# A hybrid decoder layer on eight cores: weight casts in small pieces, early tiles in idle buffers, the mix stored alone, a new memory map for phase two

## The reference

```python
h = layer_norm(concat([meta, x]), ln_emb_g, ln_emb_b)      # 16 meta tokens + 8192 tokens, 1024 wide
hq, hf, hi, hg, aq, ak, av, gates = split(h @ w_in)        # one input projection
y_hg  = hgrn2_mixer(hq, hf, hi, hg, ...) @ w_branch_hg     # gated linear recurrence, 4 heads, chunks of 128
y_att = swa_sink_attention(aq, ak, av, ...) @ w_branch_attn  # window 128, meta tokens and a sink always seen
g_hg, g_att = split(sigmoid(gates))
mix = (g_hg * y_hg + g_att * y_att) @ w_out
h = layer_norm(ALPHA * h + mix, ln1_g, ln1_b)
a, u = split(h @ w_ffn_in)                                 # 1024 -> 2 x 2816
h = layer_norm(ALPHA * h + (silu(a) * u) @ w_ffn_out, ln2_g, ln2_b)
```

## Time and profile before

| | |
|---|---|
| Three runs | 3938.48, 4109.31, 4582.92 us (median 4109.31) |
| Profiled execution | 3938.09 us |
| Its span, slowest core | 3936.5 us |
| Spans of the eight cores | 3900.2 to 3936.5 us |
| Busy share of the span | TensorE 92%, VectorE 56%, ScalarE 31%, GpSimd 23% |

### The profile page before, as it was taken

How to read it: one execution, slowest core, us unless ns; L and a number is a source line. 1 busy time by engine, 2 the same in 40 slices (tenths; PEclk the granted TensorE clock), 3 DMA queues, 4 the chain that set the end, 5 groups by cost and what they waited for, 6 DMA issues and landing times.

```text
span 3936.5 us, 46968 instructions; the slowest of 8 cores (3900.2 to 3936.5 us)
## 1 busy us (share of the span) xinstructions
PE 3629.1 (92%) x17838; PEld 1638.3 (42%) x17838; DVE 2185.5 (56%) x2962; ACT 1233.6 (31%) x1981; POOL 899.1 (23%) x907
## 2 busy tenths in 40 slices
PE   1368989999999999999988999999999999999998
PEld 0133443444444444444433444444444444444443
DVE  2476766667777777776544444434544443444433
ACT  2254444445545555555422111111111111111110
POOL 1223332333333343333221111101111110111100
PEclk8679999999999999999999999999999999999999
DMA  8746766766676666665556444455555444555532
GB/s 154 146 119 155 194 170 177 183 188 177 198 195 173 177 193 186 185 183 164 157 190 189 145 149 140 132 152 161 156 149 145 146 132 145 155 165 145 149 114 81
DMA packets 405412, 631.01 MB, mean 160 GB/s; under 512 B 270482, under 2 KB 279842, under 8 KB 403908
## 3 DMA queue, kind: packets, MB, share of 16 engines
q1 hardware_dynamic: 400628, 597.59, 52.9%
q0 software_dynamic: 4560, 30.41, 5.4%
HBM read 495.60 MB, written 126.35 MB: 158 GB/s over the span
## 4 chain that ended last, share of the span: by engine, by line
PE 74%; DMA 10%; DVE 9%; ACT 3%; issue 2%; POOL 2%; SPq 1%; DVEq 0%; POOLq 0%; ACTq 0%
PE ps L1329 27%; PE ps L1352 15%; PE ps L90 8%; PE ps L1089 8%; PE ps L947 4%; PE ps L1127 4%; PE ps L801 3%; DMA xB_78<-h_scr 2%; PE ps L1106 2%; DMA ring<-wgb_bf 2%; DMA xA_77<-x 2%; PE ps L1103 1%; PE ps L773 1%; DVE rd L90 1%; DVE m_149 L90 1%
## 5 line engine op out<-in xcount | busy, mean ns | idle before, releaser
L1352 PE MATMUL ps<-wfo,gT 128*128 128x512 bf16 x2736 | 603.6, 379 | 0.0
L1329 PE MATMUL ps<-h1T_166,ring 128*128 128x512 bf16 x2482 | 592.4, 380 | 0.0
L1329 PE MATMUL ps<-h1T_167,ring 128*128 128x512 bf16 x2480 | 590.1, 379 | 0.0
L1352 PEld LDWEIGHTS ps<-wfo,gT 128*128 128x128 bf16 x2736 | 267.7, 98 | 322.8
L1329 PEld LDWEIGHTS ps<-h1T_166,ring 128*128 128x128 bf16 x2482 | 243.4, 98 | 294.6 <-issue 3.2
L1329 PEld LDWEIGHTS ps<-h1T_167,ring 128*128 128x128 bf16 x2480 | 242.7, 98 | 292.6
L90 POOL TENSOR_SCALAR rs_54<-mv_50 128x1 f32<-128x1 f32 x32 | 40.9, 1278 | 1142.1 <-DVE mv_50 L90 1142.1
L90 POOL TENSOR_TENSOR mT<-m_149 128x512 bf16<-128x512 f32 x128 | 174.8, 1365 | 463.4 <-DVE m_149 L90 371.9
L90 DVE RECIPROCAL rd<-ps 128x512 f32<-128x512 f32 x64 | 214.3, 3348 | 38.8 <-PE ps L1063 38.7
L90 DVE TENSOR_TENSOR gT<-sl_169,ps 128x512 bf16<-128x512 f32 x128 | 87.7, 686 | 263.0 <-PE ps L1329 261.9
L90 ACT ACTIVATE sl_169<-ps 128x512 f32<-128x512 f32 x128 | 76.4, 597 | 494.1 <-PE ps L1329 494.1
(11 more groups left out here) (535 smaller groups left out, 6185.1 us busy)
## 6 DMA issues: line engine op xcount, KB each, us to landing
ring<-wfi_bf SPq DMA_DIRECT2D x352, 512.0 KB, 3.7
ring<-wgb_bf SPq DMA_DIRECT2D x128, 768.0 KB, 5.9
xA_77<-x SPq DMA_DIRECT2D x64, 512.0 KB, 5.1
h_scr<-xA_77 SPq DMA_DIRECT2D x64, 512.0 KB, 3.6
ring<-wqf_bf SPq DMA_DIRECT2D x64, 512.0 KB, 5.7
xB_78<-h_scr SPq DMA_DIRECT2D x64, 512.0 KB, 4.3
r_scr<-xB_78 SPq DMA_DIRECT2D x64, 512.0 KB, 2.8
wfi_bf<-w_fi POOLq DMA_DIRECT2D x22, 512.0 KB, 7.4
```

Of the source, the lines that this page charges most:

```text
L1329: inst = e.matmul(bank(P, k)[:, 0:ntok], w[:, c * 256 + k * 128:c * 256 + (k + 1) * 128], h1T[g % 2][:, c, 0:ntok], start=(c == 0), stop=( ...
L1352: inst = e.matmul(bank(P, n), gT[:, gslots[j], s * 128:(s + 1) * 128], wfo[:, j, n * 512:(n + 1) * 512], start=(j == 0), stop=(j == NJ - 1))
```

## The change

- A cast is split: `cast_tile` and `cast_rows` cut each weight into pieces of 256 KB of fp32 (128 KB of bf16; `wo` in pieces of twice that). Still four are in flight, now four pieces. The order is `wakv`, `waq`, two heads of `wqf`, `wv`, `whg`, the other two heads, then as before. 25 casts ahead of the FFN weights become 92, the 44 of the FFN weights 132.
- The first x tile is loaded ahead of all else. `xA` has two buffers; in the first two groups stage 0 also uses `ogT[1]` and `aoT[1]`, which are idle then, so four x tiles can be loaded at once. `hbf` and `og` fall from two buffers to one; the meta tokens' `kdm` shares `A_sb[0]`.
- Stage 5 no longer loads h: ScalarE copies the scaled product to `xB`, which is stored to `r_scr`. Stage 6 loads h and the mix (`mx`, two buffers), and GpSimd adds them.
- In a normalisation the addition of eps moves from GpSimd to VectorE (also for `ss` of the recurrence); the power stays on GpSimd.
- The map of phase two puts `h1` and `h1T` on `wv`, `whg`, `waq`, `wakv`, `th`, `qd`, and `wfo` at the end, on `wo`, `xB`, `mT` and their neighbours.
- `WIN`: stage 2 ends at 0.9, stage 5 runs from 0.5 to 0.8, stage 0 from 0.6 to 0.95.

```diff
-NXA, NXB, NHB = 1, 1, 2
+NXA, NHB, NOG = 2, 1, 1
...
-WIN = {"2": (0, 1), "3": (0, 1), "12": (0, 1), "4": (0, 0.5), "5": (0.6, 1), "0": (0.5, 1)}
+WIN = {"2": (0, 0.9), "3": (0, 1), "12": (0, 1), "4": (0, 0.5), "5": (0.5, 0.8), "0": (0.6, 0.95)}
...
+    kdm, Bkdm = A_sb[0], BA[0]
+    x0 = [(xA[0], [BxA[0]]), (xA[1], [BxA[1]]),
+          (ogT[1][:].rearrange("p h t -> p (h t)").bitcast(F32), BogT[1]),
+          (aoT[1][:].rearrange("p h t -> p (h t)").bitcast(F32), BaoT[1])]
...
+    NH1 = 8
+    h1, Bh1 = sbn("h1", [128, D], F32, NH1)
+    h1T, Bh1T = partsn("h1T", [128, 8, 512], BF16, 4, 2)
+    h1b, Bh1b = sbn("h1b", [128, D], BF16, 2)
+    mx, Bmx = sbn("mx", [128, D], F32, 2)
...
+    place["at"] = (limit - NJ * 2048) // 32 * 32
+    wfo, Bwfo = sb("wfo", [128, NJ, 1024], BF16, NJ)
...
+    def cast_tile(t, src, Bs, ncol):
+
+        n = 8 // len(Bs)
+        for k, b in enumerate(Bs):
+            cast_dma(t[:, k * n:(k + 1) * n, :].rearrange("p c n -> p (c n)"), src[:, k * n * ncol:(k + 1) * n * ncol],
+                     [b], n * ncol * 512)
+
+    def cast_rows(dst, src, Bs, ncol, after=()):
+
+        n = 128 // len(Bs)
+        for k, b in enumerate(Bs):
+            cast_dma(dst[k * n:(k + 1) * n, :], src[k * n:(k + 1) * n, :], [b], n * ncol * 4, after)
...
-        S.op("pool", lambda e: e.tensor_scalar(out=rs[i][p0:p1, :], in0=mv[i][p0:p1, 1:2], scalar1=eps, scalar2=None,
-                                               op0=ALU.add), [Bmv[i]], [Brs[i]], cost=200)
+        S.op("dve", lambda e: e.tensor_scalar(out=rs[i][p0:p1, :], in0=mv[i][p0:p1, 1:2], scalar1=eps, scalar2=None,
+                                              op0=ALU.add), [Bmv[i]], [Brs[i]], cost=160)
...
-        k = t % NXA
+        k = s if g < 2 else s % NXA
...
-        dma(lambda e: e.dma_start(out=xb[:], in_=h_d[t * 128:(t + 1) * 128, :]), [Bh_d[t]], [Bxb], "hl%d" % k, 524288)
...
-            S.op("pe", fw(n), BmT + [Bwo, Bxb], [P.sub[n]], cost=MM(8))
-        S.op("dve", lambda e: e.scalar_tensor_tensor(out=xb[:], in0=pair(P), scalar=0.5 / ALPHA, in1=xb[:],
-                                                     op0=ALU.mult, op1=ALU.add), P.sub + [Bxb], [Bxb],
-             cost=dve(1024))
+            S.op("pe", fw(n), BmT + Bwo, [P.sub[n]], cost=MM(8))
+        S.op("act", lambda e: e.activation(out=xB[:], in_=pair(P), func=AF.Copy, scale=0.5 / ALPHA), P.sub, [BxB],
+             cost=act(1024))
...
+    cast_tile(wakv, w_akv, Bwakv, 256)
+    cast_tile(waq, w_aq, Bwaq, 512)
+    cast_rows(wqf_d[0], w_qf[0], Bwqf[0], 2048)
+    cast_rows(wqf_d[1], w_qf[1], Bwqf[1], 2048)
+    cast_tile(wv, w_v, Bwv, 512)
+    cast_tile(whg, w_hg, Bwhg, 512)
+    cast_rows(wqf_d[2], w_qf[2], Bwqf[2], 2048)
+    cast_rows(wqf_d[3], w_qf[3], Bwqf[3], 2048)
...
-        dma(lambda e: e.dma_start(out=h1[k][:], in_=r_d[t * 128:(t + 1) * 128, :]), [Br_d[t]], [Bh1[k]], "r%d" % k,
+        dma(lambda e: e.dma_start(out=h1[k][:], in_=h_d[t * 128:(t + 1) * 128, :]), [Bh_d[t]], [Bh1[k]], "h%d" % k,
             524288)
-        layer_norm(h1[k], Bh1[k], G1, BG1, B1, BB1, EPS / (ALPHA * ALPHA))
+        dma(lambda e: e.dma_start(out=mx[kb][:], in_=r_d[t * 128:(t + 1) * 128, :]), [Br_d[t]], [Bmx[kb]],
+            "m%d" % kb, 524288)
+        S.op("pool", lambda e: e.tensor_tensor(out=h1[k][:], in0=h1[k][:], in1=mx[kb][:], op=ALU.add),
+             [Bh1[k], Bmx[kb]], [Bh1[k]], cost=2300)
+        layer_norm(h1[k], [Bh1[k]], G1, BG1, B1, BB1, EPS / (ALPHA * ALPHA))
```

More of the change, by code:

```diff
@@ L487, in sbn, with parts, partsn @@
         return [a for a, _ in ts], [b for _, b in ts]
+    def parts(name, shape, dt, n):
+        t, b = sb(name, shape, dt)
+        bs = [Buf("%s_%d" % (name, k), b.lo, b.hi) for k in range(n)]
+        allb[phase["n"]].remove(b)
+        allb[phase["n"]] += bs
+        return t, bs
+    def partsn(name, shape, dt, n, count):
+        ts = [parts("%s%d" % (name, i), shape, dt, n) for i in range(count)]
+        return [a for a, _ in ts], [b for _, b in ts]
     ring, Bring = sb("ring", [128, RING, 1024], BF16, RING)
@@ L700, in build, with layer_norm @@
     lnk = {0: 0, 1: 0}
-    def layer_norm(xb, Bxb, G, BG, Bt, BBt, eps, p0=0, p1=128, part=0):
+    def layer_norm(xb, Bx, G, BG, Bt, BBt, eps, p0=0, p1=128, part=0):
         i = 2 * part + lnk[part] % 2
@@ L724, in stage0 @@
     def stage0(t, g, s):
-        k = t % NXA
-        xb, Bxb = xA[k], BxA[k]
+        k = s if g < 2 else s % NXA
+        xb, Bx = x0[k]
         kb = t % NHB
-        dma(lambda e: e.dma_start(out=xb[:], in_=x[(t - 1) * 128:t * 128, :]), [], [Bxb], "x%d" % k, 524288)
-        layer_norm(xb, Bxb, Gemb, BGemb, Bemb, BBemb, EPS)
-        S.op("act", lambda e: e.copy(out=hbf[kb][:], in_=xb[:]), [Bxb], [Bhbf[kb]], cost=act(1024))
-        dma(lambda e: e.dma_start(out=h_d[t * 128:(t + 1) * 128, :], in_=xb[:]), [Bxb], [Bh_d[t]], "hs%d" % k,
+        dma(lambda e: e.dma_start(out=xb[:, :], in_=x[(t - 1) * 128:t * 128, :]), [], Bx, "x%d" % k, 524288)
@@ L733, in stage0 @@
+        layer_norm(xb, Bx, Gemb, BGemb, Bemb, BBemb, EPS)
+        S.op("act", lambda e: e.copy(out=hbf[kb][:], in_=xb[:, :]), Bx, [Bhbf[kb]], cost=act(1024))
+        dma(lambda e: e.dma_start(out=h_d[t * 128:(t + 1) * 128, :], in_=xb[:, :]), Bx, [Bh_d[t]], "hs%d" % k,
             524288)
@@ L1198, in build @@
         for p in (0, 64):
-            S.op("act", lambda e, i=i, p=p: e.copy(out=Em[i][p:p + 1, :, :].rearrange("p g q -> p (g q)"),
-                                                   in_=snk[p:p + 1, :]), [Bsnk, BEm[i]], [BEm[i]], cost=act(1024))
+            S.op("act", lambda e, i=i, p=p: e.copy(out=Em[p:p + 1, :, :].rearrange("p g q -> p (g q)"),
+                                                   in_=snk[p:p + 1, :]), [Bsnk, BEm], [BEm], cost=act(1024))
     for i in range(1):
-        E64 = Em[i][64:65, :, :].rearrange("p g q -> p (g q)")
+        E64 = Em[64:65, :, :].rearrange("p g q -> p (g q)")
@@ L1254, in build @@
     ops = S.ops
-    ops += rec(meta_tile)
-    for s, t in enumerate(groups[0]):
-        ops += rec(stage0, t, 0, s)
-        ops += rec(stage0T, t, 0, s)
+    st0 = [rec(stage0, t, 0, s) + rec(stage0T, t, 0, s) for s, t in enumerate(groups[0])]
+    ops += st0[0][:1] + setup + rec(meta_tile) + st0[0][1:] + sum(st0[1:], [])
     ops += s12(0)
```

243 lines of the change are left out of this document (91 added, 152 removed).

## The result

The changed kernel takes 3816.49 us (median of four runs, 3811.9 to 3823.39). The ratio to the kernel before is **0.9713, 95% interval [0.9665, 0.9761]**: faster, by 2.9%. The forecast of 3823 us, range 3768 to 3898, was made against the execution of 3938.09 us; the medians of the kernel before (4109.31 in the three runs shown, 4023.9 beside the changed kernel) hold executions in which one die had a lower granted clock, and the ratio leaves these out. The profiled execution of the changed kernel took 3812.42 us, 125.7 less than that of before; the forecast was 115, and the ratio gives 113 of 3938 us.

A forecast was written before the change was run, and what follows sets the result against it. TensorE's waits ahead of phase two were taken as all there is to win, the start bound by casts, then the tiles' chain. 3938 - 70 (start) - 25 (stage 5) - 20 (change of phases) = 3823 us, range 3768 to 3898.

The forecast's parts named there:

- The start: Up to the first stage 4: it comes at 205 us against 275, 70 us gained.
- I take 7.4: Weight casts at the start: each of 25 windows of 512 KB takes 7.4 us, last piece landing at about 187 us.
- not 18: From the last cast piece's landing to the first stage 4: 18 us, between bounds of 5 and 46.4.
- the change cuts the tiles' chain and makes the casts the only bound: Start: four x tiles fetched at once end the one-by-one passage through `xA`, so only the weight casts bound it.
- the engines' 158 us: Start: DMA work of casts and SP's queue in the first 180 us; decides at best bounds, about 100 us gained at most.
- Stage 5 and the even stretch: From 400 us to the change of phases: dropping the load of h gains 25 us, between 10 and 45.
- All the waits it named: TensorE, 400 to 2000 us: 24.5 us for `xB` from `h_scr` and 5.0 for VectorE's addition would go.
- the moved eps additions ... I put at nothing: Normalisations: moving eps from GpSimd to VectorE gains nothing, as GpSimd has 565 us of work in 1600.
- The change of phases: Between the phases: waits of 13.4 and 6.9 us go as `h1` lies on dead weights; 20 us gained.
- Phase two: FFN phase: 64 more loads and 64 GpSimd additions are hidden and cost nothing; its 1826.5 us stay.
- loses part of its cover: Rival for phase two: both streams load too late, 165 us more at the worst, 3988 us; chance 0.03.
- the 89 us of lead: Phase two: a group's transposes are issued 89 us before their first read, which hides the added loads and additions.

The follow-up runs named there:

- x1_late_wo: The changed kernel with the eight pieces of `wo` to be cast after the first group; the planner issued them early all the same. 0.9735 of the kernel before.
- m4_map: The changed kernel with `wfo` at the beginning of phase two's map and `h1`, `h1T` over `hT` and what follows it: 0.9711 of the kernel before.

## Why the prediction was right or wrong

**The time was right, and two of its terms were wrong in size in opposite directions.** That they cancelled is luck.

*The start: 55 us for 70.* The term's number failed in "I take 7.4": the windows took 8.4 us, which moves the last piece from 187 to 211. Some of it came back, for the first stage 4 followed 9 us behind that piece and not 18. The step behind the number failed as well, "the change cuts the tiles' chain and makes the casts the only bound". With eight in flight the casts end at 172 and stage 4 still waits until 232.8; with whole casts they end at 166.8 to 210.3 over the cores, mostly earlier than with pieces, and stage 4 comes 60 to 63 us behind them; with two x tiles it waits until 244.4. Up to the first stage 4 all these kernels move 39 to 44 MB, so the question is what leaves the engines idle. Their mean share in that time is 0.74 before, 0.86 with pieces alone, 0.97 without pieces, 0.95 with eight in flight, 0.99 with two x tiles and 1.10 in the changed kernel. Early x tiles give the engines something to do, and pieces let transposes through sooner: by the medians the pieces alone bring 24 us and the rest of the change without them 28, of 57 together. Why pieces do so is argued from the waits for transposes, not shown. The forecast's floor, "the engines' 158 us", counted too little: it was the packet time of the first 180 us of before, while the changed kernel's engines show 1.10 x 220 = 242 us of it up to its first stage 4. Packet times overlap, so this is more than the work; that the rest of its start is bound by the engines is read from the shares, and x1_late_wo, which was meant to take bytes out of it, took none.

*Stage 5 and the even stretch: 50 us for 25, by the medians 39.* All the waits it named went. Its size was sound for stage 5 as the trace of before priced it: 23 us when the loads are struck out with the order held (with the change of phases in it), 30 to 40 in the stretch when stage 5 is done alone. What failed is "the moved eps additions ... I put at nothing": undoing them alone costs 24 us in this stretch, 28 by the medians, where a neutral number of the planner moves the median by 4 to 11; the stretch is then only 8 us shorter than before by the medians (1754.6 and 1762.3). The argument was GpSimd's busy share (565 of 1600 us), and that was the wrong view: an operation of GpSimd that waits for VectorE holds up what stands behind it there, and VectorE in turn waits for that. This is read from the rows of phase two; for the stretch the place was not looked up.

*The change of phases: 21 us for 20.* Right, mechanism too: with a map of the old kind TensorE waits 20.5 us for the first `h1T`. But this price holds only in place; in m4_map most of it was made up ahead.

*Phase two: nothing, and nothing it was.* The reason, loads and additions well ahead of their readers, is only half of it. With eps on GpSimd the same loads and additions cost 39 to 60 us. The rival that phase two "loses part of its cover" was real, and it was the edit put at nothing that kept it away, not the 89 us of lead; its mechanism was not a late `h1T` but an addition that stands behind another tile's eps.

*What stays open.* Fractions, second `xA` and stage 5 cannot be given prices of their own. Each undone alone costs 51 to 107 us, each done alone in the kernel before makes it 1 to 3% slower. The one neutral push of the planner that was tried moves the time by 0.3% at most, so luck of the order is unlikely to be all of it. But the kernels with one part done kept eps on GpSimd and those with one part undone had it on VectorE. So the parts may need each other's room, or the moved eps; no run tells which.
